# Moving the token scale of two norms behind the products in a 1024-token layer stack, with alternating block pairs and narrow sums of squares

## The chip, the cores and the metric

The kernel runs on one core of one Trainium2 chip. The core has four compute engines that run their own instruction streams: TensorE (PE in the rows, with its weight loads as PEld), VectorE (DVE), ScalarE (ACT) and GpSimd (POOL). SyncE (SP) issues the DMA transfers. The engines meet through semaphores alone. The metric is device time in microseconds (us), lower is better: the median of three runs. All arrays are float32.

## The reference, cut to what matters

Two blocks of a network stand behind each other, for one sequence of 1024 tokens with 1024 channels. The first adds four mixers of one normalized and modulated input (retention D, sliding window B, stick-breaking C, a sparse attention A). The second has a mixer block, an MLP and a gated embedding. What the change touches is this:

```python
def rms_norm(x, g):                      # rms_norm_2 is the same
    y = xf * lax.rsqrt(jnp.mean(xf * xf, axis=-1, keepdims=True) + RMS_EPS)
    return (y * g.astype(jnp.float32)).astype(x.dtype)

# first block
mod = (jax.nn.silu(c) @ w_ada + b_ada)[:, None, :]
h = rms_norm(x, norm_g) * (1.0 + scale) + shift          # opening
# stick-breaking, branch C
log_beta = jax.nn.log_sigmoid(z)
log_1m = jnp.where(mask, jax.nn.log_sigmoid(-z), 0.0)
suffix = lax.cumsum(log_1m, axis=3, reverse=True) - log_1m
a = jnp.where(mask, jnp.exp(log_beta + suffix), 0.0)
# merge, per branch
term = jax.nn.sigmoid(h @ w_merge[i]) * (yi @ w_br[i])

# second block
h = h + rms_norm_2(mix, g_mix_post[i])
hn = rms_norm_2(h, g_mlp_pre[i])                          # norm ahead of the up products
ff = jnp.square(jax.nn.relu(hn @ w_up[i])) @ w_down[i]
h = h + rms_norm_2(ff, g_mlp_post[i])
gate = jax.nn.sigmoid(rms_norm_2(h, g_ple_pre[i]) @ w_ple_gate[i])   # norm ahead of the gates
e = (p[i] @ w_ple_proj[i]) * gate
h = h + rms_norm_2(e, g_ple_post[i])
```

The factor `rsqrt(mean)` of a norm is one number for a token, the same for all channels. Call it the token scale; the gain `g` is one number for a channel.

## The kernel before, in words

**Tiles.** Activations lie transposed, channels on the 128 partitions and the 1024 tokens along the free axis, so a tensor of 1024 channels is 8 chunks of 128x1024. A dense product is computed in blocks of 128 output channels. A block has a part for each chunk of its input; a part (`three`, L609) is six matmuls of 128x512: three products (input high by weight high, input low by weight high, input high by weight low, all fp32r) for each of two token halves. A block fills one PSUM tile of 128x1024, and the tiles take two slots in turn (`slot[g % 2]`). Blocks of kind F have 8 parts and one tile, M (merge gates, and the gates g of the last stage) has 10 parts and two tiles (8 parts the gate, 2 the projection), D (down products) also two.

**Weights.** SyncE loads the weights of a block into one buffer `raw` (L543). ScalarE copies them to `whi` (L1065, L1070), which rounds them, and GpSimd subtracts for the remainder `wlo` (L1429, L1432). Both have two buffers. The split of block b+1 stands at part 0 of block b, its load at part 2.

**Inputs of a block.** A normalized chunk is split the same way: ScalarE copies it to `xhi` (L1072), and the remainder `xlo` is made by VectorE or GpSimd in turn (L1760, L1435). So each chunk passes scaling on VectorE, copy, remainder, then TensorE.

**Norms.** The channels are on the partitions, so the sum of squares over channels is a TensorE product with ones. There are two forms. The narrow form (`square_sums`, L687) has the squares as the stationary operand, eight products with one column, and leaves one 128x8 tile for the 1024 tokens; root and reciprocal are then of 128x8, and `broadcast` (L715) spreads the result to a 128x1024 row in PSUM with eight 128x128 products. The wide form (`chunk_sums`, L702) has the ones as the stationary operand and the squares as 512 moving columns, and leaves the sum already spread over partitions; root and reciprocal are then of 128x1024 (L1104, L1606). Norms of a sum that is complete before use add the eight squares on GpSimd first (`add_square`) and use one narrow sum. Norms whose input has only just been made use the wide form, chunk by chunk: the opening, and the pre-norms of MLP and gates.

**The two norms of the change.** `norm3` stands between the last block x7 of the mixer output and the up products, `norm4` between the last down products and the gates g0 to g7. Each is a post-norm (scale mm, add it to the residual `res`) with a pre-norm of the new residual behind it: narrow sum, row, scaling of mm (L1612), residual additions on VectorE for even chunks (L1624) and on GpSimd for odd ones (L1457), squares, wide sums, wide root and reciprocal, scaling of `res` with gain and token scale, split, first block. For the gates, ScalarE takes Sigmoid straight out of PSUM (L1238, L1239) and VectorE multiplies with the projection.

**Opening.** The same, with the input in place of the residual and with the modulation (`mod`), whose two vectors are products of `silu(c)` with `w_ada` (`ada_products`, VectorE, L1955; `modulation`, TensorE, L948).

**Order.** One list, TIMELINE (`list_timeline`, L192), is read by all engines: each goes through the same events and issues what is its own there. Between dense parts stand the events of attention (`spread`, L110, weighs them out). `number_tiles` (L247) numbers the PSUM tiles in the order of the blocks. In the stick stage ScalarE alternates between Exp (`ska`, L1272; `skt`, L1277) and Ln (`skt`, L1279), two functions in different table sets.

## Time and profile before

| | |
|---|---|
| median of three runs | 2966.54 us (2966.51 to 2966.85) |
| the profiled execution | 2968.03 us, of which the span in the profile is 2966.3 us |
| TensorE busy | 2697.6 us, 91% |
| VectorE, ScalarE, GpSimd busy | 949.6, 932.4, 878.7 us (32, 31, 30%) |
| chain that ended last | TensorE 79%, VectorE 9%, GpSimd 4%, ScalarE 3%, issue 3%, DMA 1% |
| copy of a block's weights to high (L1070) | 1100 ns mean |
| remainder of a block's weights (L1432) | 2531 ns mean |
| VectorE, one operation on a PSUM tile 128x1024 (L1733, L1722) | 1225 ns |
| transfers | 134.81 MB, 45 GB/s mean |

The shares of busy time are means over stages that differ. In the page's row of forty slices TensorE's busy tenths are 4 and 7 in the first two, and 6 in four later ones. The order in which to read is: the table of stretches for where TensorE idles, the chain for what a stretch costs it, and the timeline for what each engine waited for there.

### The profile page before, as it was taken

To read this page: it belongs to the slowest core of one execution; us is meant where nothing else is said; L and a number is where in the kernel's file an instruction comes from. 1 tells how busy PE (TensorE), PEld (TensorE's weight loads), DVE (VectorE), ACT (ScalarE), POOL (GpSimd) and SP (SyncE) were. 2 spreads that over 40 slices of the span, in tenths; PEclk is the share of its full clock that TensorE was granted. 3 is DMA by queue.
4 is the path that set the end of the run, shared out by engine and by line. 5 is a ranking of instruction groups with operands and counts; after the bars stand their busy time and mean duration, and the time that the engine had idled before them with its cause. 6 is when DMAs were issued, how large, how long until landed. Compare 5 with 4: busy or idle time off the path is not lost.

```text
span 2966.3 us, 29752 instructions
## 1 busy us (share of the span) xinstructions
PE 2697.6 (91%) x12244; PEld 2125.0 (72%) x12244; DVE 949.6 (32%) x1423; ACT 932.4 (31%) x1308; POOL 878.7 (30%) x497
## 2 busy tenths in 40 slices
PE   4799999999998999999988999696999999999696
PEld 2677778666687777788777777473888888888475
DVE  6212440233202454511237564406022222222512
ACT  3102441688721344421332333223211111112221
POOL 1212111343321111133642121243333322334343
PEclk9888999999997899999989999898999999999798
DMA  6101011100011000011221000110111111111011
GB/s 266 43 22 41 27 33 43 36 18 18 15 50 42 18 19 10 15 44 42 100 74 62 15 29 27 54 67 8 50 50 50 43 50 50 50 50 43 32 45 66
DMA packets 33431, 134.81 MB, mean 45 GB/s; under 512 B 3536, under 2 KB 3856, under 8 KB 32400
## 3 DMA queue, kind: packets, MB, share of 16 engines
q1 hardware_dynamic: 32976, 131.85, 12.7%
q8 instruction: 98, 1.61, 0.2%
q10 hardware_dynamic: 320, 1.05, 0.1%
q14 instruction: 37, 0.30, 0.0%
HBM read 123.45 MB, written 8.39 MB: 44 GB/s over the span
## 4 chain that ended last, share of the span: by engine, by line
PE 79%; DVE 9%; POOL 4%; ACT 3%; issue 3%; DMA 1%; SPq 0%; POOLq 0%; ACTq 0%; DVEq 0%
PE slot L613 48%; PE slot L658 12%; PE ps L826 4%; PE ps L797 3%; DVE mm L1612 2%; PE ps L775 2%; PE ps L859 1%; PE ps L850 1%; POOL wlo L1432 1%; PE ps L863 1%; PE ps L876 1%; DVE cacc L2015 1%; POOL xlo L1439 1%; DMA mm<-xT 1%; POOL pbuf L1446 1%
## 5 line engine op out<-in xcount | busy, mean ns | idle before, releaser
L613 PE MATMUL slot<-xhi,whi 128*128 128x512 f32 x2192 | 720.5, 411 | 95.8 <-DVE xlo L1764 32.9
L613 PE MATMUL slot<-xlo,whi 128*128 128x512 f32 x2192 | 693.8, 398 | 0.0
L613 PE MATMUL slot<-xhi,wlo 128*128 128x512 f32 x2192 | 690.2, 397 | 0.0
L1432 POOL TENSOR_TENSOR wlo<-raw,whi 128x1024 fp32r<-128x1024 f32 (+1 forms) x169 | 427.7, 2531 | 766.5 <-ACT whi L1070 766.5
L613 PEld LDWEIGHTS slot<-xhi,whi 128*128 128x128 f32 x2192 | 407.4, 194 | 196.0 <-issue 83.7
L613 PEld LDWEIGHTS slot<-xlo,whi 128*128 128x128 f32 x2192 | 423.3, 193 | 92.9
L613 PEld LDWEIGHTS slot<-xhi,wlo 128*128 128x128 f32 x2192 | 421.5, 192 | 92.4
L1070 ACT ACTIVATE whi<-raw 128x1024 fp32r<-128x1024 f32 (+1 forms) x169 | 185.9, 1100 | 276.4 <-PE slot L658 174.5
L658 PE MATMUL slot<-uhi,whi 128*128 128x512 f32 x512 | 158.3, 390 | 0.0
L658 PE MATMUL slot<-ulo,whi 128*128 128x512 f32 x512 | 157.8, 389 | 0.0
L658 PE MATMUL slot<-uhi,wlo 128*128 128x512 f32 x512 | 157.6, 389 | 0.0
L1507 POOL TENSOR_TENSOR ulo<-tbuf,uhi 128x1024 fp32r<-128x1024 f32 x32 | 76.6, 2395 | 226.9 <-ACT uhi L1217 226.9
L1733 DVE TENSOR_TENSOR mm<-slot,mm 128x1024 f32<-128x1024 f32 x56 | 68.6, 1225 | 229.3 <-PE slot L658 228.3
L797 PEld LDWEIGHTS ps<-brv,pbuf 128*128 128x128 f32 x936 | 127.0, 196 | 19.6 <-ACT cb L1308 5.8
L1722 DVE TENSOR_SCALAR tbuf<-slot 128x1024 f32<-128x1024 f32 x32 | 39.2, 1225 | 316.5 <-PE slot L613 316.5
L1252 ACT ACTIVATE pbuf<-ps 128x512 f32<-128x512 f32 (+3 forms) x176 | 79.5, 452 | 174.8 <-PE ps L775 173.3
L1217 ACT ACTIVATE uhi<-tbuf 128x1024 fp32r<-128x1024 f32 x32 | 33.9, 1060 | 304.3 <-DVE tbuf L1724 304.3
L1493 POOL TENSOR_TENSOR mm<-mm,zs 128x1024 f32<-128x1024 f32 x24 | 58.0, 2416 | 237.4 <-DVE zs L1646 237.4
L797 PE MATMUL ps<-brv,pbuf 128*128 128x64 f32 x936 | 122.1, 273 | 5.6 <-ACT cb L1308 3.3
L658 PEld LDWEIGHTS slot<-uhi,whi 128*128 128x128 f32 x512 | 95.5, 188 | 22.3 <-issue 3.0
L658 PEld LDWEIGHTS slot<-uhi,wlo 128*128 128x128 f32 x512 | 96.1, 188 | 20.2
L658 PEld LDWEIGHTS slot<-ulo,whi 128*128 128x128 f32 x512 | 96.1, 188 | 20.1
(301 smaller groups left out, 3223.0 us busy)
## 6 DMA issues: line engine op xcount, KB each, us to landing
raw<-wstream SPq DMA_DIRECT2D x129, 512.0 KB, 3.2
raw<-wstream SPq DMA_DIRECT2D x40, 640.0 KB, 3.8
ada<-wada SPq DMA_DIRECT2D x6, 2048.0 KB, 30.3
mm<-xT SPq DMA_DIRECT2D x1, 4096.0 KB, 24.0
mm<-xT SPq DMA_DIRECT2D x8, 512.0 KB, 3.8
res_dram<-mm SPq DMA_DIRECT2D x8, 512.0 KB, 6.2
res<-res_dram SPq DMA_DIRECT2D x8, 512.0 KB, 6.6
outT<-res SPq DMA_DIRECT2D x8, 512.0 KB, 2.6
```

Of the source, the lines that this page charges most:

```text
L613: o = mm_(outs[:, half * HALF:(half + 1) * HALF], w[b % 2][:, k_w, :], x[:, k_x, half * HALF:(half + 1) * HALF], start=first and j == 0, s ...
L658: o = mm_(slot[(g + t) % 2][:, half * HALF:(half + 1) * HALF], w[:, kc, t, :], x[:, kc, half * HALF:(half + 1) * HALF], start=kc == 0 and ...
L775: o = nc.tensor.transpose(ps6[:, (c - 4 * bi) * P:(c - 4 * bi + 1) * P], sring[m % 3][:, c * P:(c + 1) * P], t_("ident"))
L797: o = mm_(ps7[:, 0:DH], ptr[:, c * P:(c + 1) * P], v, start=c == 0, stop=c == nb - 1)
L826: o = mm_(ps4[:, c0:c1], q_[r0:r0 + DH, :], k_[r0:r0 + DH, lo * P + c0:lo * P + c1], start=j == 0, stop=j == 2)
L1070: nc.scalar.activation(flat(whi[b % 2])[:, 0:n], raw[:, 0:n], ACT.Copy).then_inc(w_hi, 1)
L1252: nc.scalar.activation(ptr[:, bi * HALF:bi * HALF + w], ps6[:, 0:w], ACT.Copy).then_inc(s_ptsb, 1)
L1432: tt(flat(wlo[b % 2])[:, 0:n], raw[:, 0:n], flat(whi[b % 2])[:, 0:n].bitcast(F32), ALU.subtract).then_inc(w_lo, 1)
L1493: tt(mm[:, n, :], mm[:, n, :], zs[0][:], ALU.add).then_inc(sum_done, 1)
L1507: tt(ulo[:, n, :], tbuf[n % 2][:], uhi[:, n, :].bitcast(F32), ALU.subtract).then_inc(u_lo, 1)
L1612: v.scalar_tensor_tensor(out=dst, in0=src, scalar=g, in1=row, op0=ALU.mult, op1=ALU.mult).then_inc(s_, 1)
L1733: v.tensor_tensor(mm[:, n, :], slot[gg % 2][:], mm[:, n, :], ALU.add).then_inc(slot_free[gg % 2], 1)
```

## The change

What it does, in five parts:

1. **Pairs.** The first two blocks behind a norm are issued alternately: part i of the first, then part i of the second for i up to 3, then the rest. The pairs are Dv0/Dv1, o0/o1, Ecb0/Eca0, x0/x1, u0_0/u0_1 and g0/g1 (`opened`, `opened_gates`). The weights of the second block are split at the norm instead of at part 0 of the first, and those of block 1 are loaded right behind those of block 0 (ahead of the tables and of the last modulation weights). The residual's load moves from part 0 of x1 to part 3. The tiles of g0 and g1 are renumbered: g0 has tiles t and t+2, g1 has t+1 and t+3.
2. **Token scale behind the products.** In `norm3` and `norm4` the chunks that go into the products carry the gain alone: `xhi` is a ScalarE copy of `res` scaled by the gain, `xlo` a VectorE operation with gain and subtraction, and all eight residual additions are GpSimd's. The squares of the chunks are summed in narrow form, one after each of the eight rounds of the pair (`hsum`); root, reciprocal and the row (`hrow`, ahead of the second block's last two parts) follow while products run. The row is copied to `wide_row`. For the up blocks the evacuation becomes max(x, 0) times the row. For the gates VectorE multiplies tile by row (`scale_gate`, at part 7), ScalarE takes Sigmoid of that in place, and VectorE multiplies with the projection.
3. **Sums.** All sums of squares are in narrow form. The sums of a complete tensor take two accumulators: GpSimd's sum of seven, and the last square straight from ScalarE.
4. **Opening.** Chunk sums in narrow form, root and reciprocal of 128x8, then the row by eight products. VectorE's reciprocal stands between its product 3 and 4 of the modulation's second half. Chunk squares use three buffers in place of two.
5. **Tables.** `preload_act_table_set("natural_log_exp_and_others")` at the start of the stick stage and behind each gate Sigmoid of branch B: one set that holds both functions.

Where the order moves, from the instruction streams of the two kernels. First TensorE in the opening, ahead of the first weight block (L948 and L986 are the modulation, sbuf and pbuf hold squares, slot is a block's tile). Before:

```order
L948 MATMUL ps<-tab,ada_sum_102 128x1 x8
L709 MATMUL ps<-sbuf_72,tab 128x512 x2
L709 MATMUL ps<-sbuf_73,tab 128x512 x2
L709 MATMUL ps<-sbuf_72,tab 128x512 x2
L709 MATMUL ps<-sbuf_73,tab 128x512 x2
L709 MATMUL ps<-sbuf_72,tab 128x512 x2
L709 MATMUL ps<-sbuf_73,tab 128x512 x2
L709 MATMUL ps<-sbuf_72,tab 128x512 x2
L709 MATMUL ps<-sbuf_73,tab 128x512 x2
L948 MATMUL ps<-tab,ada_sum_101 128x1 x8
L613 MATMUL slot<-xhi,whi_56 128x512 x2
```

After:

```order
L986 MATMUL ps<-tab,ada_sum_102 128x1 x8
L731 MATMUL ps<-tab,sbuf_72 128x1 x8
L731 MATMUL ps<-tab,sbuf_73 128x1 x8
L731 MATMUL ps<-tab,pbuf_74 128x1 x8
L731 MATMUL ps<-tab,sbuf_72 128x1 x8
L731 MATMUL ps<-tab,sbuf_73 128x1 x8
L731 MATMUL ps<-tab,pbuf_74 128x1 x8
L731 MATMUL ps<-tab,sbuf_72 128x1 x8
L731 MATMUL ps<-tab,sbuf_73 128x1 x8
L757 MATMUL ps<-tab,rrms 128x128 x8
L986 MATMUL ps<-tab,ada_sum_101 128x1 x8
L653 MATMUL slot<-xhi,whi_56 128x512 x2
```

The eight wide matmuls are eight groups of eight one-column ones, and the row's broadcast stands ahead of the second modulation.

Next TensorE at the norm ahead of the up products, from the row's sum on (whi_57 and whi_56 are the weights of u0_0 and u0_1). Before:

```order
L690 MATMUL ps<-tab,pbuf_74 128x1 x8
L720 MATMUL ps<-tab,rrms 128x128 x8
L709 MATMUL ps<-sbuf_72,tab 128x512 x2
L709 MATMUL ps<-sbuf_73,tab 128x512 x2
L709 MATMUL ps<-sbuf_72,tab 128x512 x2
L709 MATMUL ps<-sbuf_73,tab 128x512 x2
L709 MATMUL ps<-sbuf_72,tab 128x512 x2
L709 MATMUL ps<-sbuf_73,tab 128x512 x2
L709 MATMUL ps<-sbuf_72,tab 128x512 x2
L709 MATMUL ps<-sbuf_73,tab 128x512 x2
L613 MATMUL slot<-xhi,whi_57 128x512 x2
L613 MATMUL slot<-xlo,whi_57 128x512 x2
```

After:

```order
L731 MATMUL ps<-tab,pbuf_74 128x1 x8
L731 MATMUL ps<-tab,sbuf_73 128x1 x8
L757 MATMUL ps<-tab,rrms 128x128 x8
L653 MATMUL slot<-xhi,whi_57 128x512 x2
L653 MATMUL slot<-xlo,whi_57 128x512 x2
L653 MATMUL slot<-xhi,wlo_59 128x512 x2
L653 MATMUL slot<-xhi,whi_56 128x512 x2
L653 MATMUL slot<-xlo,whi_56 128x512 x2
L653 MATMUL slot<-xhi,wlo_58 128x512 x2
L731 MATMUL ps<-tab,sbuf_72 128x1 x8
L653 MATMUL slot<-xhi,whi_57 128x512 x2
L653 MATMUL slot<-xlo,whi_57 128x512 x2
```

The eight wide sums that stood ahead of the first product are gone from there; behind each round of the two blocks stands a narrow sum.

Last ScalarE in the stick stage, about a Sigmoid of the merge gates (zs). Before:

```order
L1272 ACT_TABLE_LOAD
L1272 ACTIVATE ska_81<-ps 128x128
L1277 ACTIVATE skt_79<-skt_79 128x384
L1279 ACT_TABLE_LOAD
L1279 ACTIVATE skt_79<-skt_79 128x384
L1169 ACT_TABLE_LOAD
L1169 ACTIVATE zs_108<-slot 128x1024
L1070 ACTIVATE whi_56<-raw 128x1280
L1272 ACT_TABLE_LOAD
L1272 ACTIVATE ska_82<-ps 128x256
L1277 ACTIVATE skt_80<-skt_80 128x512
L1279 ACT_TABLE_LOAD
```

After:

```order
L1303 ACTIVATE ska_81<-ps 128x128
L1308 ACTIVATE skt_79<-skt_79 128x384
L1310 ACTIVATE skt_79<-skt_79 128x384
L1203 ACT_TABLE_LOAD
L1203 ACTIVATE zs_108<-slot 128x1024
L1205 ACT_TABLE_LOAD
L1112 ACTIVATE whi_56<-raw 128x1280
L1303 ACTIVATE ska_82<-ps 128x256
L1308 ACTIVATE skt_80<-skt_80 128x512
```

The table loads at every change between Exp and Ln are gone; a Sigmoid has its own load ahead of it and one behind it. In all the built program has 154 table loads before and 67 after.

The diff, cut to its core:

```diff
+OPENERS = [("Dv0", "Dv1"), ("o0", "o1"), ("Ecb0", "Eca0"), ("x0", "x1"), ("u0_0", "u0_1")]
+SECOND = {b for _, b in OPENERS} | {"g1"}
...
+def opened(events, a, b):
+
+    first, second = dense_part_events([a]), dense_part_events([b])
+    at = events.index(first[0])
+    rest = [ev for ev in events if ev not in first and ev not in second]
+    pair = []
+    for i, ev in enumerate(first):
+        pair.append(ev)
+        if i < 4:
+            pair.append(second[i])
+        if a == "u0_0":
+            pair.append(("hsum", 4, i))
+    pair += second[4:]
+    if a == "u0_0":
+        pair.insert(-2, ("hrow", 4))
+    return rest[:at] + pair + rest[at:]
...
+def opened_gates(events):
+
+    g0, g1 = dense_part_events(["g0"]), dense_part_events(["g1"])
+    at = events.index(g0[0])
+    rest = [ev for ev in events if ev not in g0 and ev not in g1]
+    pair = []
+    for i in range(8):
+        pair.append(g0[i])
+        if i < 4:
+            pair.append(g1[i])
+        pair.append(("hsum", 6, i))
+    pair += g1[4:6] + [("hrow", 6)] + g1[6:8] + g0[8:] + g1[8:]
+    return rest[:at] + pair + rest[at:]
...
+            g += {"g0": 1, "g1": 3}.get(name, 2 if kind in "MD" else 1)
...
+            load_weights(1)
...
+            def column_sum(k, accs, place=0):
+
                 if place == 0:
                     pe.wait_ge(nstd, k)
-                square_sums(place, acc, place == 0, True).then_inc(nsum, 1)
-
-            def chunk_sums(k, j):
-
-                if k:
+                for m, (acc, sem_, n) in enumerate(accs):
+                    pe.wait_ge(sem_, n)
+                    o = square_sums(place, acc, place == 0 and m == 0, m == len(accs) - 1)
+                o.then_inc(nsum, 1)
+
+            def chunk_sum(k, j, n):
+
+                if k and n == 0:
                     pe.wait_ge(nstd, k)
-                for n in range(NC):
-                    pe.wait_ge(pq_done, 8 * j + n + 1)
-                    for half in range(2):
-                        o = mm_(sum_banks(k)[half], t_("ones"), sbuf[n % 2][:, half * HALF:(half + 1) * HALF],
-                                start=n == 0, stop=n == 7)
-                    if n < 7:
-                        o.then_inc(pq_used, 1)
-                o.then_inc(nsum, 1)
+                pe.wait_ge(pq_done, 8 * j + n + 1)
+                square_sums(0, sring[n % 3], n == 0, n == 7).then_inc(pq_used if n < 7 else nsum, 1)
...
             modulation(1)
-            chunk_sums(0, 0)
+            for n in range(NC):
+                chunk_sum(0, 0, n)
+            broadcast(0)
             modulation(0).then_inc(mod_mm, 1)
...
+                        act.preload_act_table_set("natural_log_exp_and_others")
...
+                    if ev[2] == 7 and BLOCKS[ev[1]][1][0] == "g":
+                        n = int(BLOCKS[ev[1]][1][1])
+                        act.wait_ge(g_scaled, n + 1)
+                        nc.scalar.activation(zs2[n % 2][:], zs2[n % 2][:], ACT.Sigmoid).then_inc(g_sig, 1)
...
+                    wait_tile(act, LAST_USE[4 if k == 3 else 5])
+                    split_weights(INDEX["u0_1" if k == 3 else "g1"])
                     for n in range(NC):
                         wait_residual(act, int(k == 5), n)
+                        nc.scalar.activation(xhi[:, n, :], res[:, n, :], ACT.Copy,
+                                             scale=v_("g_mlp_pre" if k == 3 else "g_ple_pre", n, 1)).then_inc(x_hi, 1)
                         chunk_square(1 if k == 3 else 2, n, res[:, n, :])
-                    std(k + 1)
-                    wait_tile(act, LAST_USE[4 if k == 3 else 5])
-                    for n in range(NC):
-                        act.wait_ge(x_src, 16 + 8 * (k == 5) + n + 1)
-                        split_wide(n, mm[:, n, :])
                     if k == 5:
                         act.wait_ge(p_in, 32)
                         for n in range(2):
                             nc.scalar.activation(yhi[:, n, :], zs2[n][:], ACT.Copy).then_inc(y_hi, 1)
+                    std(k + 1)
...
+            def add_residual(k, n):
+                pool.wait_ge(t_ready, 8 * k + n + 1)
+                tt(res[:, n, :], res[:, n, :], mm[:, n, :], ALU.add).then_inc(res_odd if n % 2 else res_added, 1)
...
-                    v.tensor_scalar(t[:], slot[g % 2][:], 0.0, None, ALU.max).then_inc(slot_free[g % 2], 1)
+                    v.scalar_tensor_tensor(out=t[:], in0=slot[g % 2][:], scalar=0.0, in1=wide_row,
+                                           op0=ALU.max, op1=ALU.mult).then_inc(slot_free[g % 2], 1)
...
+            def scale_gate(name):
+
+                n, g = int(name[1]), TILE[name]
+                wait_tile(dve, g)
+                if n < 2:
+                    dve.wait_ge(y_lo, 10)
+                v.tensor_tensor(zs2[n % 2][:], slot[g % 2][:], wide_row, ALU.mult).then_inc(slot_free[g % 2], 1)
+                wait_evacuated(dve, name)
+                v.tensor_copy(token[:, 0:1], token[:, 1:2]).then_inc(g_scaled, 1)
...
+                    if (t, kc) == (0, 4):
+                        dve.wait_ge(nstd, 1)
+                        v.reciprocal(rrms[:, 0, :], rms[:, 0, :]).then_inc(nrstd, 1)
...
-                    add_residual(k, (k - 3) // 2, post)
-                    applied(k, t_ready, 8 * (k - 1) // 2)
-                    row = rstd(k + 1)
-                    for n in range(NC + 1):
+                    row, first = rstd(k), 8 * (4 if k == 3 else 5)
+                    for n in range(NC + 2):
                         if n < NC:
-                            wait_residual(dve, (k - 3) // 2, n)
-                            scaled(mm[:, n, :], res[:, n, :], v_(pre, n, 1), row, x_src)
-                        if n:
-                            split_wide(4 if k == 3 else 5, n - 1, n - 1, mm[:, n - 1, :])
-                    applied(k + 1, x_src, 24 + 4 * (k - 3))
+                            scaled(mm[:, n, :], mm[:, n, :], v_(post, n, 1), row, t_ready)
+                        if n == NC:
+                            applied(k, t_ready, 8 * (k - 1) // 2)
+                        m = n - 2
+                        if m >= 0:
+                            dve.wait_ge(x_hi, first + m + 1)
+                            v.scalar_tensor_tensor(out=xlo[:, m, :], in0=res[:, m, :], scalar=v_(pre, m, 1),
+                                                   in1=xhi[:, m, :].bitcast(F32), op0=ALU.mult, op1=ALU.subtract
+                                                   ).then_inc(x_lo if m % 2 else x_lo2, 1)
+                    v.tensor_copy(wide_row, rstd(k + 1)).then_inc(napplied, 1)
+                    dve.wait_ge(napplied, k + 2)
```

## Rows read from the trace of the kernel before

**Rows 1.** Table of stretches: stretch and us, busy us of each engine, clock, DMA, GB/s.

```profile
core 0: us, PE busy (x) PEld busy (x) DVE busy (x) ACT busy (x) POOL busy (x), PEclk, DMA share, GB/s
555.00:800.00 245.00, 237.21 (x947) 153.82 (x948) 75.65 (x132) 204.84 (x247) 98.81 (x109) 0.97 0.06 21
1527.00:1540.00 13.00, 11.77 (x56) 9.01 (x56) 7.62 (x8) 7.90 (x8) 9.54 (x4) 1.00 0.01 1
1999.00:2066.00 67.00, 38.12 (x111) 22.27 (x110) 45.29 (x28) 22.15 (x23) 22.23 (x9) 0.80 0.02 6
2758.00:2830.00 72.00, 39.60 (x114) 22.77 (x112) 46.51 (x29) 22.57 (x23) 28.76 (x11) 0.79 0.07 24
```

**Rows 2.** The chain that ended last: start us, length us, engine, tile, line.

```profile
27.79 16.04 PE ps L709 x32
...
79.68 11.20 PE slot L613 x48
...
2070.50 32.92 PE slot L613 x144
...
2147.02 43.52 PE slot L613 x192
...
2830.39 99.81 PE slot L613 x432
```

**Rows 3.** Timeline of the opening: start, length, operation, in brackets the idle before.

```profile
22.44 3.54 PE L948 MATMUL ps<-tab,ada_sum 128*128 128x1 f32 x16 [22.44 <-DVE ada_sum L1955]
...
36.56 5.25 DVE L1955 SCALAR_TENSOR_TENSOR ada_sum<-ada,csil,ada_sum 128x1024 f32<-128x1024 f32 x4 [0.26 <-DMA ada<-wada]
...
43.66 1.84 PE L948 MATMUL ps<-tab,ada_sum 128*128 128x1 f32 x16
...
52.83 2.48 DVE L2026 SCALAR_TENSOR_TENSOR mm<-mm,gmul,pbuf 128x1024 f32<-128x1024 f32 x2
```

**Rows 4.** Table of stretches: mixed work behind a wait; narrow products alone.

```profile
578.00:588.20 10.20, 9.25 (x19) 5.93 (x20) 2.86 (x4) 5.53 (x7) 6.46 (x4) 0.50 0.17 49
919.00:926.20 7.20, 7.20 (x72) 7.13 (x71) 0.00 (x0) 0.02 (x1) 0.00 (x0) 0.50 0.22 86
```

**Rows 5.** Groups by line and form, ScalarE, 540 to 810: busy and mean ns, idle before.

```profile
L1279 ACT ACT_TABLE_LOAD x48 | 61.6, 1283 | 0.9
```

**Rows 6.** Timeline of the stick stage, TensorE behind a Sigmoid.

```profile
578.95 1.19 PE L613 MATMUL slot<-xhi,whi 128*128 128x512 f32 x2 [3.38 <-ACT zs L1169]
...
779.70 1.19 PE L613 MATMUL slot<-xhi,whi 128*128 128x512 f32 x2 [3.75 <-ACT zs L1169]
```

**Rows 7.** Waits, 555 to 800: engine, line, waited for: total us, times, longest.

```profile
PE ps L859 <- DVE skt L1848: 2.1, 1, 2.1
```

**Rows 8.** Timeline about the second norm and the mixer output (x0, x1).

```profile
1538.51 1.95 PE L720 MATMUL ps<-tab,rrms 128*128 128x128 f32 x16
...
1893.55 3.31 DVE L1703 TENSOR_TENSOR zs<-zs 128x1020 f32<-128x1020 f32 x1
...
1932.03 1.06 ACT L1070 ACTIVATE whi<-raw 128x1024 fp32r<-128x1024 f32 x1 [6.07 <-DMA raw<-wstream]
```

**Rows 9.** Timeline of the norm ahead of the up products.

```profile
2005.79 3.58 PE L690 MATMUL ps<-tab,pbuf 128*128 128x1 f32 x16 [4.62 <-POOL pbuf L1446]
...
2009.96 3.78 PE L720 MATMUL ps<-tab,rrms 128*128 128x128 f32 x16 [0.59 <-DVE rrms L1603]
...
2017.59 2.35 POOL L1457 TENSOR_TENSOR res<-res,mm 128x1024 f32<-128x1024 f32 x1 [11.85 <-DVE mm L1612]
2018.73 2.28 DVE L1624 TENSOR_TENSOR res<-res,mm 128x1024 f32<-128x1024 f32 x1
...
2038.50 6.55 DVE L1606 RECIPROCAL pbuf<-pbuf 128x1024 f32<-128x1024 f32 x1 [6.70 <-ACT pbuf L1104]
```

**Rows 10.** Timeline of the norm ahead of the gates, and of the last norm.

```profile
2767.43 3.78 PE L720 MATMUL ps<-tab,rrms 128*128 128x128 f32 x16 [0.73 <-DVE rrms L1603]
...
2935.01 3.57 PE L690 MATMUL ps<-tab,pbuf 128*128 128x1 f32 x16 [4.82 <-POOL pbuf L1446]
```

164 lines of the change are left out of this document (79 added, 85 removed).

## The prediction

> **What bounds the kernel now.** I read the table of stages first. In it the reader sees which stages leave TensorE idle: 28.9 us of the 67 ahead of the MLP and 32.4 us of the 72 behind it are idle, while the stage of the stick-breaking attention (555 to 800) has only 7.8 idle in 245 though ScalarE is busy for 205 [rows 1]. So TensorE is the bound everywhere but in the norms. The chain of waits comes next, for the price of a block: four blocks of 8 parts take 43.52 us, 10.88 each, 1.36 us a part at full clock [rows 2]. Then the order of time at each norm shows what ends last.
>
> **Opening.** Now the eight chunk sums are 16.04 us of TensorE [rows 2], the first scaled chunk starts at 52.83 [rows 3], and the second block starts at 79.68 and takes about 11.0, to 90.7 [rows 2]. After, a chunk sum is eight products with one column. The same form takes 3.54 us in the cold and 1.84 just behind wide products [rows 3]. Which of the two holds is the first question. The trace has 7.2 us of nothing but narrow products, TensorE and its weight loads busy all the time, and the clock is granted at 0.50 throughout, 1.2 GHz of 2.4 [rows 4]. So I take the cold price: 8 x 3.44 (3.54 less the overlap) = 27.5, from 27.8 to 55.4. Root and reciprocal end at 56.0. VectorE has held back four of its products behind that reciprocal, 5.25 us [rows 3], to 61.4; the modulation's products follow cold, 3.54, to 65.0, and 0.9 of small operations: the first scaled chunk is at 65.9, 13 later than now. The row of the root stands in PSUM then, so scaling shares no port with GpSimd's subtractions; and the second block's first four parts fill the gaps between chunks. First product 3.9 later, 12 products at 1.2 GHz 5.1, then 13 us to the end of the first block's part 7 and 5.5 for the second's last four with what the gaps cost: 28.1, so the pair ends at 94.0. **Term: +3.3.** If the sums ran at 1.84 the same steps give 52.2 + 28.1 = 80.3, -10.4; that is the other end.
>
> The Trainium skill ("TensorE: Matmul & The Clock Gate", section "What's actually happening") says that sustained matmul activity releases the throttle, whatever the number of products. By it the narrow sums would warm up as the wide ones did. This trace speaks against it for narrow ones; I keep it as a rival. By the rows the whole change comes to -59.4, by the rule to 13.7 less, -73.1.
>
> **Stick-breaking attention.** The built program has 154 table loads before and 67 after; the 95 that alternate between exp and log (48 of them here [rows 5], 1.28 us each) become one at the start and one behind each gate's Sigmoid. Nearly all of that lies under TensorE, which is the bound there. What it can return are the places where TensorE waits: 3.38 us at 578.95 and 3.75 at 779.70, both for a Sigmoid that stands behind a log load and its own [rows 6]. One load less there, and a shorter queue ahead, gives 1.9 and 1.4; one wait of 2.1 for VectorE's mask behind a log [rows 7] gives about 1.3. The first wait also drops the clock, for some 10 us of mixed work [rows 4], worth 5, and the second one for 3.4, worth 1.7. With all of the clock it is 11.3, with none 4.6. **Term: -9.**
>
> **Other pairs.** For o0/o1, GpSimd's weight remainder (2.4) now stands ahead of its four chunk remainders, and TensorE waits for it instead of for the chunk: 0, within 1. For the pair after the second norm the idle time between chunks is filled (1.2 idle in 13 us [rows 1], 2 over the whole pair), and the doubled narrow sums (four for two) start 4.8 earlier and end 0.3 earlier: **-2.3**. For x0/x1 the third weight block no longer waits behind the residual's load (GpSimd's weight remainder there ended 1.7 us after TensorE was free; ScalarE shows the wait for the DMA [rows 8]): -1.7; but GpSimd gets one more operation in the stretch where VectorE is already stopped by each (3.31 for a 1.22 operation [rows 8]): +2.2, on the path to the wait for the pool product. **+0.5**, from -1.7 to +2.5.
>
> **Norm ahead of the up products.** Now: x7 ends at 2001.2; sum starts 4.62 later, row broadcast at 2009.96 for 3.78, ready 2013.8; residual, chunk sums, a wide reciprocal of 6.55 [rows 9], scaling, and the second block starts at 2070.50 [rows 2], ends 2081.45. After, step by step:
> - ScalarE squares x7 from PSUM, 1.06; the sum of the other seven starts at once, warm 1.8, then the last square's 1.8, behind wide products. Root, reciprocal: row broadcast at 2005.7, cold 3.8: T0 = 2009.45, 4.3 earlier.
> - GpSimd adds all eight chunks, 2.35 each. In the rows VectorE's two-operand SBUF addition of 1.22 takes 2.28 beside it [rows 9]: the two exclude each other. VectorE's remainder (1.2) is such an operation, so a chunk costs 3.5, the first is ready at T0 + 7.2, the last by +32.
> - TensorE: at 1.2 GHz the first pair takes 5.1, its sum 2.0; then three rounds of two parts and a sum, 2.72 + 1.8 = 4.55; four of one part and a sum, 3.2: the last sum ends at +41.0. The chunks come faster than that from the second on, so TensorE sets the time, and between narrow sums it has wide parts enough that I take the full clock. Two parts 2.8, the row 1.8 warm (1.95 at 1538.51 [rows 8]), two parts 2.7: the second block ends at T0 + 48.3 = 2057.8.
> - The row's copy (1.22) and the first scaled evacuation (1.28) end at +47.9, just under the last two parts; third block's weights at +44.9. In the MLP the scaling adds 0.06 to a VectorE operation that waits for TensorE: nothing.
>
> **Term: 2057.8 - 2081.45 = -23.7.** The stages behind need no new wait.
>
> **Norm ahead of the gate products.** T0 comes from 2771.25 (the broadcast at 2767.43 plus 3.8 [rows 10]) to 2767.1, 4.15 earlier. The same 48.3; then the projection parts of g0 and g1, 2.75 each, to +53.8. GpSimd's narrow remainders, for which TensorE waits now, are done by +38. One wait is new: ScalarE must split g2's weights before g0's Sigmoid, and that split waits for g0's second tile at +51.0. Then 1.26, a table load 1.28, Sigmoid 1.03, the product 1.23 (what such operations take on these engines), gaps 0.3: g2 starts at +56.1, 2.3 after TensorE is free, = 2823.2. Now g2 starts 6 x 13.6 before the end of 2830.39 + 99.81 [rows 2], at 2848.5. **-25.3.** The other six gates run as now: scaling frees the first slot 1.3 us after its tile, the other tile takes 2.7.
>
> **Tail.** The sum of the first seven is ready, the last square comes 2.75 after TensorE's end instead of 4.82 of wait [rows 10] for GpSimd as well; two sums instead of one. First row of the result 2.0 to 3.6 earlier: **-2.9**.
>
> **Sum:** 3.3 - 9 - 2.3 + 0.5 - 23.7 - 25.3 - 2.9 = -59.4. The profiled execution took 2968.03 with a span of 2966.3; less 59.4 it is 2908.6, and 2907.1 from the median of 2966.54, which I predict as 2907.
>
> **Rivals.**
> - Narrow sums warm the clock in the opening (10.4 gained, not 3.3 lost): 2893.4. For it: the same form ran in 1.84 in this very place now, if behind wide products [rows 3]. Against: the clock of 0.50 under narrow products alone [rows 4]. 7%.
> - The eight additions and eight remainders hold each other up as the scalings and subtractions do now, a chunk each 5.6 us instead of 3.5: the last remainder at +46, then sum, two parts, row, two parts: 57, 8.7 later in both norms: 2907.1 + 17.4 = 2924.5. For it: all eight additions are now on the slower engine. Against: the blocked operation waits for one partner only. 12%.
> - Table loads don't pay (TensorE is full there): 2907.1 + 4.4 = 2911.5, inside the forecast.
> - Slower: a clock that narrow sums among wide parts hold at 1.2 GHz, at both pairs. Rounds then cost 5.12 + 3.44 and 2.56 + 3.44: 34.2 + 24.0 after +7.3, four parts 10.2 and the row 3.8: +79.5 where now it is +72.0, so 7.5 lost, and 8.3 lost before g2; the mixed rows of the stick stage stay slow too, 4.6 gained only. 3.3 - 4.6 - 2.3 + 0.5 + 7.5 + 8.3 - 2.9 = +9.8: 2976.3. It decides from where both pairs are in the low state for over 70% of their time. For it: the same row [rows 4]. Against: each round has a part or two of six wide products. 4%.
>
> **Numbers.** Forecast 75% (2898 to 2917), warm opening 7%, slow chunks 12%, slow clock 4%; 2% for something unseen. Range 2893 to 2927. A change of 0.2% is 5.9 us, about what a measurement tells from none. Faster 0.95, same 0.02, slower 0.03.
>
> **What would show it.** Eight narrow sums at 3.4 each with the clock at 0.50 in the opening, and the first scaled chunk near 66. Second block of the pair ended at 48 behind the row in both norms, no TensorE wait over 1 us in them but the first, clock 1.00 from about 5 us in. g2 2.3 us late. About 20 ScalarE table loads in the stick stage, its length 236. It is wrong if TensorE waits for remainders of a chunk past the second, or if the narrow sums inside the pairs are at 3.4.

## The result, and the profile after

The changed kernel takes 2914.81 us, the median of 4 runs from 2913.77 to 2916.03, against 2966.69 (2966.51 to 2970.18) for the kernel before in the same session. The ratio is 0.9818 with a 95% interval of 0.9806 to 0.983: 52 us gained where 59.4 were predicted (2907), inside the range of 2893 to 2927. The profiled execution has a span of 2913.8 us, 52.5 less than before, so 6.9 of the 59.4 are missing in it.

To see where it came from I cut both traces at ten points that both kernels have, the starts of ScalarE's copies of the weights of ten blocks, and took the difference of each of the eleven stages. In the same stages I added up from the clock records how long TensorE's clock was at its low level. The records begin at 31.9 us before and at 60.3 after, so what was low ahead of that is not in the first row.

| stage | before, low | after, low | change | forecast |
|---|---|---|---|---|
| start to Dk1 (opening) | 91.8, 13.7 | 95.9, 10.2 | +4.1 | +3.3 |
| Dk1 to Bm2 (retention, sliding window, first steps of stick-breaking) | 486.9, 68.9 | 483.5, 61.4 | -3.4 | 0 |
| Bm2 to Aq0 (stick-breaking) | 249.0, 13.0 | 243.2, 6.8 | -5.8 | -9 |
| Aq0 to Cm7 (A's attention) | 365.8, 81.9 | 368.0, 81.9 | +2.2 | 0 |
| Cm7 to o3 | 247.3, 6.8 | 247.4, 3.4 | +0.2 | 0 |
| o3 to Ek1 (second norm) | 212.5, 30.7 | 210.0, 30.7 | -2.6 | -2.3 |
| Ek1 to Ep1 (forgetting attention) | 193.2, 10.2 | 198.7, 20.5 | +5.5 | 0 |
| Ep1 to x4 | 102.3, 27.3 | 101.2, 27.3 | -1.1 | +0.5 |
| x4 to d0_0 (norm ahead of up) | 147.2, 27.3 | 123.2, 13.7 | -24.0 | -23.7 |
| d0_0 to g3 (norm ahead of gates) | 754.8, 34.1 | 730.5, 13.7 | -24.3 | -25.3 |
| g3 to the end | 115.4, 29.6 | 112.2, 27.2 | -3.2 | -2.9 |

From x4 on, the two late norms and the tail gave 51.5 where the sum has 51.9. Of the 6.9 that are missing, 6.5 lie ahead of x4: 1.0 was gained there where the sum has 7.5. Most of that is in attention stages whose work on TensorE the change leaves as it is.

First the opening, in the timeline of the changed kernel (start, length, operation, idle before):

```profile
34.71 3.55 PE L731 MATMUL ps<-tab,pbuf 128*128 128x1 f32 x16
...
55.86 7.16 DVE L2006 SCALAR_TENSOR_TENSOR ada_sum<-ada,csil,ada_sum 128x1024 f32<-128x1024 f32 x4
...
55.99 3.79 PE L757 MATMUL ps<-tab,rrms 128*128 128x128 f32 x16 [0.66 <-DVE rrms L1999]
...
63.07 2.98 PE L986 MATMUL ps<-tab,ada_sum 128*128 128x1 f32 x16 [3.29 <-DVE ada_sum L2006]
...
71.16 1.19 PE L653 MATMUL slot<-xhi,whi 128*128 128x512 f32 x2 [5.12 <-DVE xlo L2086]
...
94.36 1.04 PE L717 MATMUL slot<-tab,zs 128*128 128x128 f32 x8
```

A narrow sum takes 3.55 us by itself and 3.44 in the row of eight, and the pair is done at 94.36 where 94.0 was forecast. That the two agree so well is in part luck: VectorE's four products behind the reciprocal took 7.16 and not 5.25 (one of them takes 3.26 in the chain of waits, while GpSimd makes the weight remainder below), so the first scaled chunk came at 67.17 and not at 65.9, and from there the pair took 27.2 and not 28.1.

```profile
56.66 2.63 POOL L1472 TENSOR_TENSOR wlo<-raw,whi 128x1024 fp32r<-128x1024 f32 x1 [56.15 <-ACT whi L1112]
```

The chain of waits answers to the wide sums of [rows 2] with one piece, which holds all eight sums:

```profile
27.87 27.48 PE ps L731 x128
...
71.16 23.38 PE slot L653 x96
```

Three signs were named wrongly. The stick stage was to take 236 us with about 20 table loads of ScalarE; from Bm2 to Aq0 it takes 243.2, with 14 (90 before). And I had said that the clock column would read 0.50 in the opening. It reads 1.00, because this trace has no clock record before 60 us:

```profile
28.00:55.00 27.00, 27.00 (x128) 27.00 (x128) 4.61 (x4) 8.27 (x8) 0.00 (x0) 1.00 0.31 132
64.00:74.00 10.00, 4.88 (x17) 4.25 (x18) 7.59 (x10) 5.06 (x6) 4.35 (x2) 0.50 0.98 325
```

The durations tell the level: 3.55 for the form that takes 1.84 at the high clock [rows 3]. So the clock was low through 27 us of narrow products with TensorE busy all the time. In the kernel before, the first record, at 31.9 us, is a high one, 4.1 us into the wide sums. The Trainium skill ("TensorE: Matmul & The Clock Gate", section "What's actually happening") has it that activity releases the throttle; for these narrow products the trace disagrees.

The norm ahead of the up products, against [rows 9]:

```profile
2000.24 1.84 PE L731 MATMUL ps<-tab,pbuf 128*128 128x1 f32 x16
...
2001.94 3.03 PE L731 MATMUL ps<-tab,sbuf 128*128 128x1 f32 x16
...
2005.56 3.78 PE L757 MATMUL ps<-tab,rrms 128*128 128x128 f32 x16 [0.59 <-DVE rrms L1645]
...
2010.81 24.62 POOL L1494 TENSOR_TENSOR res<-res,mm 128x1024 f32<-128x1024 f32 x8 [2.17 <-DVE mm L1651]
...
2014.37 2.17 DVE L2130 SCALAR_TENSOR_TENSOR xlo<-res,vec,xhi 128x1024 fp32r<-128x1024 f32 x1 [1.32 <-ACT xhi L1432]
...
2016.69 1.19 PE L653 MATMUL slot<-xhi,whi 128*128 128x512 f32 x2 [7.35 <-DVE xlo L2130]
...
2020.87 1.84 PE L731 MATMUL ps<-tab,sbuf 128*128 128x1 f32 x16
```

The first sum stands right behind x7 instead of 4.62 us later. The second one is slower than worked out, 3.03 and not 1.8: the clock records have the low level from 2002.5 on. So the row starts 5.2 behind x7's end where it was 8.8, 3.6 sooner and not 4.3. The first product comes 7.35 behind the row, the clock is high again from 2019.6, and TensorE waits for nothing more: the pair ends 47.0 behind the row (48.3 forecast), because the clock rose 2.9 us into the pair and not after 5. GpSimd's eight additions and VectorE's remainders give a chunk about every 3.3 us (3.5 was worked out); the "slow chunks" rival (5.6) is out, and so is the slow clock: sums among wide parts take 1.84. The wait at the gates came too, 2.49 where 2.3 was forecast:

```profile
2793.35 1.27 ACT L1112 ACTIVATE whi<-raw 128x1280 fp32r<-128x1280 f32 x1 [10.04 <-PE slot L653]
...
2794.64 1.28 ACT L1326 ACT_TABLE_LOAD   x1
...
2797.09 1.22 DVE L1777 TENSOR_TENSOR mm<-slot,zs 128x1024 f32<-128x1024 f32 x1 [5.21 <-ACT zs L1326]
...
2798.46 0.70 PE L653 MATMUL slot<-xhi,whi 128*128 128x512 f32 x2 [2.49 <-DVE mm L1777]
```

In the stick stage the two waits of [rows 6] are 1.49 and 2.48 now, and the wait for VectorE of [rows 7] has stayed, where 1.3 of it was to go:

```profile
578.20 0.70 PE L653 MATMUL slot<-xhi,whi 128*128 128x512 f32 x2 [1.49 <-ACT zs L1203]
```

```profile
772.74 0.70 PE L653 MATMUL slot<-xhi,whi 128*128 128x512 f32 x2 [2.48 <-ACT zs L1203]
```

```profile
PE ps L897 <- DVE skt L1896: 2.1, 1, 2.1
```

### The profile page after: what moved, and what is told of

The parts are those of the page before. It is cut to its first block, busy times and chain, and to the rows that moved or that the text cites. A ratio compares the mean times of both kernels' runs of the same rounds, so it can differ in the third digit from the quotient of the medians.

```text
span 2913.8 us, 30462 instructions
## 1 busy us (share of the span) xinstructions
PE 2709.8 (93%) x12660; PEld 2179.4 (75%) x12660; DVE 922.2 (32%) x1431; ACT 817.1 (28%) x1218; POOL 872.8 (30%) x492
## 4 chain that ended last, share of the span: by engine, by line
PE 87%; DVE 6%; ACT 3%; POOL 2%; issue 2%; DMA 1%; SPq 0%; POOLq 0%; ACTq 0%; DVEq 0%
PE slot L653 54%; PE slot L699 12%; PE ps L864 4%; PE ps L835 3%; PE ps L731 3%; PE ps L813 2%; PE ps L897 1%; PE ps L888 1%; PE ps L901 1%; PE ps L914 1%; DVE cacc L2068 1%; DMA mm<-xT 1%; DVE ada_sum L2006 1%; PE ps L757 1%; POOL wlo L1472 1%
## 5 line engine op out<-in xcount | busy, mean ns | idle before, releaser
L1759 DVE SCALAR_TENSOR_TENSOR tbuf<-slot,tab 128x1024 f32<-128x1024 f32 x32 | 39.2, 1224 | 302.4 <-PE slot L653 302.3
```

## The experiments

Eleven runs: the changed kernel once more, and ten further versions. The kernel before was run beside each group: medians of 2968.2 to 2968.7, with single runs between 2965 and 2978. Single runs of one kernel lie up to 14 us apart, so a difference of a few us between two medians says little; what an edit did is read from the stages. Stage lengths below are from one profile each.

| run | us, median (range) | ratio to before, 95% |
|---|---|---|
| e1_again | 2919.8 (2913.8 to 2921.5) | 0.9828 (0.9814 to 0.9841) |
| e2_tables_off | 2928.4 (2920.4 to 2932.4) | 0.9851 (0.9836 to 0.9866) |
| e3_tables_only | 2971.8 (2960.2 to 2974.5) | 1.0002 (0.9991 to 1.0012) |
| e4_ug_in_row | 2929.6 (2924.6 to 2936.8) | 0.9866 (0.9849 to 0.9883) |
| e5_late_by_3 | 2916.1 (2915.6 to 2917.1) | 0.9821 (0.9808 to 0.9835) |
| e6_sigmoid_first | 2914.8 (2914.2 to 2916.7) | 0.9817 (0.9804 to 0.9831) |
| e7_even_on_vector | 2923.0 (2922.0 to 2925.5) | 0.9844 (0.9831 to 0.9858) |
| e8_pair_sums | 2904.7 (2901.2 to 2908.8) | 0.9783 (0.9767 to 0.9798) |
| e9_rounded_sums | 2887.6 (2886.1 to 2892.4) | 0.9724 (0.971 to 0.9738) |
| e10_combined | 2881.7 (2880.0 to 2888.0) | 0.9707 (0.9691 to 0.9723) |
| e11_before_late | 2973.2 (2969.6 to 2978.4) | 1.0016 (1.0007 to 1.0025) |

### Where the 6.5 us missing ahead of x4 went: e1, e2, e3, e5, e11

Two theories are tried here. Theory P (phase): the records of TensorE's clock change only at the points of one even raster, which has no fixed place in the program, and what a short wait costs depends on where it lies against that raster. "0.45 us behind a point" below is the distance of a stage's start from the last such point. Rival C (the change): something that the change leaves behind makes the stages longer.

**e1_again**, no edit.

> The changed kernel as it is, once more. Open is why the stages between the opening and the mixer's output gave 1.0 us in the first profile where the prediction has 7.5: by the first profile the sparse attention of branch A (blocks Cm2 to Cm7) was 2.4 us longer than before and the forgetting attention (Ek1 to Ep1) 5.5 us longer, though not an instruction of theirs was changed. Theory P (phase): TensorE's clock falls and rises on a grid of its own, and these stages have short waits that cost one interval or two, as they fall on it; then this execution may show either length, and the time is 2914.8 within 2. Rival C (the change): something that the change leaves behind makes the stages longer, the forgetting attention is 198 to 199 us from the copy of Ek1's weights to that of Ep1's here as well, 193.2 before. A time of 2913 to 2917 by both.

The stages repeat: A's attention from Cm2 to Cm7 233.5 (233.6 in the first profile, 231.1 before), the forgetting attention 198.5. That fits both theories, since both executions started the forgetting attention 0.45 us behind a point of the raster. The median was 5 higher than in the first session, with one run at 2913.8; the profiled execution was longer in the opening, from Dk1 to Bm2, from d0_0 to g3 and in the last stage, 1.3 to 1.7 us each.

**e2_tables_off** takes the two requests for the table set out of the changed kernel, and **e3_tables_only** puts the same lines into the kernel before.

```diff
                     if name[0] == "B":
-                        act.preload_act_table_set("natural_log_exp_and_others")
 ...
-                if s == 0:
-                    act.preload_act_table_set("natural_log_exp_and_others")
```

> The changed kernel without its two requests for the exp/log table set (part 5 undone, all else stays). By the first profile, stick-breaking gave 5.8 us from block Bm2 to Aq0 instead of 9. Theory: the waits for two Sigmoids are 1.3 to 1.9 us longer again, and the clock falls for 10 us behind the first: 5.8 us are lost in the stick stage, 2920.6, and between 2919 and 2923 with what the other attention stages make of the new phase. Rival: table loads lie under TensorE and pay for nothing but what the two waits show directly, 2.3 us, 2917. Rival: my forecast of 9 was right and was lost again behind the stage: 2924. Theory P also says: as everything behind the stick stage moves by an amount that is no multiple of the clock's interval, the forgetting attention takes a different length than in e1_again (193 to 199 us); rival C says it stays.

> The kernel before with the two requests for the exp/log table set and nothing else. Theory: 4.6 to 8 us gained in the stick stage, so 2959 to 2962. Rival (table loads hidden under TensorE): within 1.5 us of before, 2965 or more. Rival C about the forgetting attention: if the table set left behind were its cause, that stage would be 198 us instead of 193.2 here too, and the gain would all but vanish, 2964 to 2966; theory P leaves it anywhere from 193 to 199.

The table of stretches, from Bm2 to Aq0, of e1, e2 and e3:

```profile
581.90:825.08 243.18, 240.71 (x979) 157.62 (x979) 74.74 (x121) 96.38 (x156) 98.09 (x97) 0.99 0.06 21
```

```profile
582.93:831.85 248.92, 244.58 (x983) 160.68 (x984) 73.04 (x121) 193.73 (x232) 97.91 (x97) 0.97 0.06 20
```

```profile
577.63:820.80 243.17, 240.70 (x979) 157.59 (x979) 74.72 (x121) 96.37 (x156) 98.09 (x97) 0.99 0.06 21
```

ScalarE's busy time halves, from 193.7 to 96.4, and the stage gives 5.7 to 5.8 of it, the same in both kernels. The first steps of stick-breaking stand ahead of Bm2, and 12 of the table loads with them: there the requests give 0.5 more (Bm1 to Bm2 29.5 for 30.0). My theory of 5.8 holds for the stage, neither rival does. For the whole it does not: the median of e2, 2928.4, is above all three forecasts, and e3 took 5.8 us out of the kernel before and is no faster (its span 2.7 longer), because its forgetting attention took 200.2 instead of 193.2 and A's attention 233.6 instead of 231.1. In the changed kernel the same edit is worth 8.7 by the medians (e2 against e1) and 10.8 by the profiled spans, the stage's 5.7 and 3.8 between Cm7 and o3 (251.2 against 247.4) among it. So much of the price of an edit was set behind it. Without the requests the forgetting attention was at its longest, 200.7: the table set left behind is not the cause there. For A's attention these two runs can't tell: it took 231.1 to 231.2 in the three profiles without the requests and 233.5 to 233.6 in nine of the ten with them, and the starts differ in the same way, 2.0 to 2.1 and 2.3 to 2.4 us behind a point. The tenth speaks for the start: e8 changes the opening alone, starts this stage 3.2 behind a point and takes 236.1. Before, after, e8:

```profile
962.40:1193.52 231.12, 215.25 (x1136) 173.44 (x1136) 106.67 (x280) 99.18 (x204) 39.15 (x35) 0.90 0.05 15
```

```profile
957.01:1190.56 233.55, 217.55 (x1136) 175.27 (x1136) 106.15 (x280) 99.20 (x203) 39.16 (x35) 0.89 0.04 15
```

```profile
947.78:1183.84 236.06, 219.98 (x1136) 176.85 (x1136) 106.12 (x280) 99.36 (x204) 39.20 (x35) 0.88 0.04 15
```

**e5_late_by_3** and **e11_before_late** add the same work to the changed kernel and to the kernel before.

```diff
+                if name == "Ek1" and part == 0:
+                    for _ in range(14):
+                        mm_(slot[g % 2][:, 0:HALF], whi[b % 2][:, 0, :], xhi[:, 0, 0:HALF], start=True, stop=True)
```

> The changed kernel with 14 extra products of 128x512 (0.227 us each, 3.2 us in all, overwritten at once) in TensorE's stream at the head of block Ek1, just ahead of the forgetting attention. [...] 3.2 us later the changed kernel stands at 0.45 + 3.2 - 3.41 = 0.2, so the stage is near the short length, 193.2 to 195.5 plus the 3.2 of extra work: 196.4 to 198.7, no longer than the 198.5 without it, though 3.2 us of work were added. Rival C (the change has made the stage longer by itself): 198.5 + 3.2 = 201.7. The whole time follows: 2916 to 2920 by P, 2922 to 2923 by C, against the 2919.8 of e1_again.

> The kernel before with the same 14 extra products (3.2 us) at the head of block Ek1 that cost the changed kernel nothing in e5_late_by_3. Theory P (what counts is where the forgetting attention lies against the clock's grid): the kernel before starts it 0.07 us behind a point of the grid, its shortest place (193.2 us). 3.2 us later is 3.2 behind a point, where e2 and e3 (3.34 and 3.10) took 200.7 and 200.2: 200.2 to 200.7 and the 3.2 of work, 203.4 to 204, so the same 3.2 us of work cost 10 here, and the kernel takes 2975 to 2979. Rival (the extra wide products kept TensorE busy in e5 and so shortened the low stretch by themselves): they would do so here as well, and the stage would be no longer than 193.2 + 3.2 = 196.4, the kernel at most 3.2 slower, 2970 to 2972.

The starts that both expectations speak of, in the profiles up to then: 0.07 us behind a point in the kernel before (193.2 us), 0.45, 0.45 and 0.49 in the changed kernel, e1 and e4 (198.4 to 198.7), 3.10 and 3.34 in e3 and e2 (200.2 and 200.7). In the sum for e5 the 3.2 us carry the start past the next point, from where the distance counts anew. The stretch from Ek1 to Ep1, the kernel before first, then the changed kernel, e5 and e11:

```profile
1653.33:1846.53 193.20, 183.51 (x986) 146.19 (x986) 106.25 (x184) 66.15 (x143) 33.07 (x34) 0.97 0.07 25
```

```profile
1647.99:1846.69 198.70, 189.06 (x988) 150.54 (x988) 106.21 (x184) 66.15 (x143) 33.05 (x34) 0.95 0.08 24
```

```profile
1647.77:1846.16 198.39, 188.75 (x1002) 150.19 (x1001) 106.22 (x184) 66.13 (x142) 33.13 (x34) 0.97 0.07 24
```

```profile
1652.82:1854.87 202.05, 192.40 (x1003) 153.22 (x1003) 106.37 (x185) 66.19 (x143) 33.18 (x34) 0.95 0.07 24
```

In this stage 14 more products cost the changed kernel nothing, and the kernel before 8.9 us. What they change is the clock. Far behind them, at the second low stretch of the stage, the changed kernel has it low for two steps in a row and e5 for one:

```profile
1726.05:1729.46 3.41, 3.24 (x15) 3.24 (x16) 2.32 (x3) 0.31 (x2) 0.59 (x1) 0.50 0.48 154
1729.46:1732.87 3.41, 3.41 (x14) 2.67 (x13) 1.89 (x5) 1.67 (x5) 0.10 (x1) 0.50 0.00 0
```

```profile
1729.20:1732.61 3.41, 3.41 (x15) 2.68 (x13) 2.34 (x7) 1.67 (x5) 0.04 (x1) 0.51 0.13 52
1732.61:1736.03 3.42, 3.42 (x24) 3.06 (x23) 0.08 (x1) 0.00 (x0) 0.42 (x1) 0.99 0.00 0
```

The stage has three places where waits and narrow products let the clock fall. In these records it falls and rises at points that are not tied to the program, and a place costs one step or two as it lies against them (in e3 and e2, which start 3.10 and 3.34 us behind a point, the second place costs three). The extra products stand ahead of the first place only and end 57 us ahead of the second, too far to have kept TensorE busy there; and in e11 they made the low time longer (20.5 against 10.2). For the forgetting attention theory P is shown, rival C and the rival of e11 are out: shifted to the start that the changed kernel has, the kernel before takes the changed kernel's length. My number for e11 was 1.5 too high: this execution came to the stage 0.68 us behind a point of the clock instead of 0.07. The 3.2 us of work take it past the next point to 0.44, where the stage took 197.8 to 198.8 in eight other profiles; 198.8 + 3.2 = 202.0, and 202.05 was measured. The Trainium skill says as much ("TensorE: Matmul & The Clock Gate", section "What's actually happening"): what watches TensorE runs freely and does not start with the kernel. It speaks there of a kernel's first products and puts the cost of their warm-up under 1% of a typical span; here the effect comes in the middle of the kernel and is 5.5 us in one stage, a tenth of what the change brings.

In e11 the whole time is a weaker witness: its median is 5.0 above the kernel before, 2973.2, between what the rival gives (up to 2972) and what P gives (2975 or more), with single runs from 2969.6 to 2978.4.

### What bounds the late pairs: e4, e7, e6

**e4_ug_in_row**.

```diff
-        if i < 4:
+        if i < 4 and a != "u0_0":
             pair.append(second[i])
 ...
-    pair += second[4:]
+    pair += second if a == "u0_0" else second[4:]
```

and the same for g0 and g1.

> The changed kernel with the blocks of the two late pairs (u0_0 then u0_1, g0 then g1) in a row instead of alternating; the narrow sums stay one behind each part of the first block, and the row stays ahead of the second block's last two parts. Theory (TensorE is the bound of the pair from the second chunk on: 16 parts 21.8, eight sums 14.7, a row 1.95 and the cold start 2.4 fill it): one part and a sum take 3.2 us and a chunk comes every 3.3, so the first block ends at about 34 to 36 behind the row and the second 12.8 later, 47 to 49 us as with alternation (48.4 measured): within 1.5 us a norm, 2912 to 2918. Rival: alternation is what fills the wait for chunks, and without it four parts (5.4 us) are lost in each norm: 2925.6. Rival: with one part a round narrow products prevail and the clock falls: a round 6.0 instead of 3.2, over 15 us a norm lost: 2945.

Ahead of the up products both blocks end 47.0 behind the row, as with alternation: for the pair itself the theory holds, and neither rival does. But the kernel takes 2929.6, well outside the theory's 2912 to 2918 (by the time alone, the rival with 2925.6 would have seemed right). The stage is 9.3 us longer, and TensorE waits behind the pair:

```profile
2060.12 1.06 ACT L1250 ACTIVATE uhi<-tbuf 128x1024 fp32r<-128x1024 f32 x1 [13.57 <-DVE tbuf L1760]
2061.09 1.04 ACT L1110 ACTIVATE whi<-raw 128x1024 fp32r<-128x1024 f32 x1
...
2064.65 2.33 POOL L1470 TENSOR_TENSOR wlo<-raw,whi 128x1024 fp32r<-128x1024 f32 x1
...
2067.04 1.22 PE L651 MATMUL slot<-xhi,whi 128*128 128x512 f32 x2 [7.97 <-POOL wlo L1470]
```

With the blocks in a row, the split of the third block's weights comes behind the evacuation of u0_0 in ScalarE's and GpSimd's streams, and that evacuation now waits for the row. I had not seen this. Ahead of the up products alternation is worth 0 by filling gaps and 9 by where it puts the next block's weights: a wait of 8.0, and a clock that is low for 20.5 us of the stage instead of 13.7. At the gates it is worth nothing in this profile: the stage up to g3 takes 731.1 (730.5 and 731.9 in the two profiles of the changed kernel), and the last one 110.8 (112.2 and 113.9).

**e7_even_on_vector**.

```diff
                             scaled(mm[:, n, :], mm[:, n, :], v_(post, n, 1), row, t_ready)
+                            if n % 2 == 0:
+                                dve.wait_ge(t_ready, 8 * ((k - 3) // 2) + n + 1)
+                                v.tensor_tensor(res[:, n, :], res[:, n, :], mm[:, n, :], ALU.add
+                                                ).then_inc(res_added, 1)
```

> The changed kernel with the residual additions of the even chunks back on VectorE, in both late norms (GpSimd keeps the odd ones), all else as changed. In the profile of the changed kernel a chunk comes every 3.3 us: GpSimd's addition 2.35, and VectorE's remainder, held until it ends. Theory (TensorE sets the pair's time from the second chunk on): only the first chunk matters, VectorE adds it in 1.2 instead of GpSimd in 2.35, so the first product comes 1.1 us sooner and each pair ends 1.1 sooner, 2.2 in all. Rival (VectorE becomes the bound: per two chunks it has two scalings, an addition, and two remainders of which each waits for GpSimd, 2.5 + 1.2 + 4.4 = 8.1 us against 6.6 now): later chunks come every 4.0 us and the pair ends 2 to 4 us later.

Slower by 2.3 in the stage ahead of up and by 1.3 to 2.7 in the next. That is the rival's amount, but by another mechanism than either had:

```profile
2017.00 2.35 DVE L2129 TENSOR_TENSOR res<-res,mm 128x1024 f32<-128x1024 f32 x1
...
2019.27 1.27 DVE L2136 SCALAR_TENSOR_TENSOR xlo<-res,vec,xhi 128x1024 fp32r<-128x1024 f32 x1
...
2020.69 1.19 PE L653 MATMUL slot<-xhi,whi 128*128 128x512 f32 x2 [8.69 <-DVE xlo L2136]
```

The first chunk is added sooner, but its remainder stands behind the third chunk's addition in VectorE's stream, and that takes 2.35 beside GpSimd's: the first product comes 8.69 behind the row, not 7.35, and the clock is low for 17.1 us of the stage, not 13.7. Afterwards TensorE waits for nothing, so the later chunks were no bound. The median is 8 above that of the changed kernel in the first session; the two stages explain 4 to 5 of it.

**e6_sigmoid_first**.

```diff
-                    if ev[2] == 0 and ev[1] + 1 < nblocks and BLOCKS[ev[1] + 1][1] not in SECOND:
+                    if (ev[2] == 0 and ev[1] + 1 < nblocks and BLOCKS[ev[1] + 1][1] not in SECOND
+                            and BLOCKS[ev[1]][1] != "g1"):
 ...
                         nc.scalar.activation(zs2[n % 2][:], zs2[n % 2][:], ACT.Sigmoid).then_inc(g_sig, 1)
+                        if n == 1:
+                            split_weights(ev[1] + 1)
```

> The changed kernel with one move: ScalarE splits the weights of g2 behind the Sigmoids of g0 and g1 instead of ahead of them. In the profile of the changed kernel g2's first product waits 2.5 us for VectorE's product of g0, which waits for that Sigmoid. Theory: the Sigmoid of g0 is done at +1.1 behind VectorE's scaling, before TensorE is through with g1, and the wait for the product goes to under 0.5 us; g2's weights then end last, 4.2 us behind the end of g0's second tile, that is before g1's second tile is through: 2.0 to 2.5 us gained in the stage. Rival: the split then comes after the second Sigmoid and g2 waits for its weights instead (GpSimd's remainder takes 2.9 behind the copy's 1.3): nothing gained, within 0.5 us.

```profile
2797.33 0.73 PE L653 MATMUL slot<-xhi,whi 128*128 128x512 f32 x2 [1.70 <-POOL wlo L1475]
```

The Sigmoid is out of the way, and GpSimd's remainder of g2's weights is what ends last: a wait of 1.70 instead of 2.49. The stage is 1.3 shorter, between theory and rival; the whole time shows nothing of it. In the changed kernel that remainder had ended only 0.8 ahead of the first product.

### What the narrow sums cost: e8, e9, e10

**e8_pair_sums**, the opening alone; the diff shows the two main parts.

```diff
-            for n in range(NC):
-                chunk_sum(0, 0, n)
-            broadcast(0)
+            for n in range(4):
+                pe.wait_ge(pp_added, n + 1)
+                square_sums(0, (sbuf[0], pbuf[0])[n % 2], n == 0, n == 3).then_inc(pp_used if n < 3 else nsum, 1)
             modulation(0).then_inc(mod_mm, 1)
+            broadcast(0)
 ...
+            for n in range(4):
+                pool.wait_ge(pq_done, 2 * n + 2)
+                a, b_ = sbuf if n % 2 == 0 else pbuf
+                tt(a[:], a[:], b_[:], ALU.add).then_inc(pp_added, 1)
```

> The changed kernel with another opening: GpSimd, idle there, adds the squares of two chunks (2.4 us each), TensorE takes four narrow sums instead of eight, VectorE's last four modulation products stand ahead of the reciprocal, and the second modulation ahead of the row. Theory (narrow sums at 3.44 us each in the cold bound the opening, 27.5 us in the profile of the changed kernel): sums from 31.1 to 44.9 at 3.44 each, modulation to 48.4, row to 52.2, first product at about 56 to 57 instead of 71.2, 14 to 15 us gained at the first product and 13 to 15 at the end of the pair: 2903 to 2906. Rival: the first weight block, whose remainder GpSimd makes behind its additions, and the load of the second block behind that, come last, and the second block waits: 10 gained. Rival: the sums are not the bound but the modulation's weights (they land at 31.6 and 36.5) with VectorE's eight products, done at 42: 10 or less.

```profile
58.98 1.19 PE L654 MATMUL slot<-xhi,whi 128*128 128x512 f32 x2 [4.99 <-DVE xlo L2096]
```

The first product came at 58.98 instead of 71.16, 12.2 sooner, and the opening stage took 84.7 instead of 95.9: 11.2 gained, between the theory's 13 to 15 and the 10 of the rivals. Two of GpSimd's additions took 3.2 to 3.3 us beside VectorE's products, and the sums ended at 46.9, not 44.9. VectorE's own eight products ended at 46.9 too, so with four sums the two are level and the sums are no longer the only bound. The edit moves several things at once; that the eight sums bounded the opening is shown better by e9, which changes them alone. The median of 2904.7 fits the theory's 2903 to 2906, but the single runs lie between 2901.2 and 2908.8, and in the profiled one, the longest, A's attention takes 2.5 more than in the changed kernel.

**e9_rounded_sums**, opening and both late norms.

```diff
-                nc.scalar.activation(sring[n % 3][:], src, ACT.Square).then_inc(pq_done, 1)
+                nc.scalar.activation(sring_r[n % 3][:], src, ACT.Square).then_inc(pq_done, 1)
 ...
+                one, step = (ones_r[:], 2) if rounded else (t_("ones", 0, 1), 1)
```

> The changed kernel with the chunk squares of the opening and of the two late norms written by ScalarE as fp32r, and summed by fp32r products with two columns of ones instead of fp32 with one (the squares are rounded, nothing else). Theory (a narrow sum costs its weight loads: fp32 takes two passes of eight, 3.44 us in the cold and 1.84 warm, and fp32r one): 1.7 us cold and 0.9 warm. Opening: eight sums 14 instead of 27.5, so the row is at 43 and VectorE's last four modulation products end last, at 48, with modulation and scaling the first product is at 56 instead of 71.2: 14 to 15 gained. In each late norm chunks, one every 3.3 us, set the pair's time: it ends 40 to 42 us behind the row instead of 47: 5 to 7 gained each. In all 24 to 29 less than 2915 to 2920, with 6 for what the clock does in the attention stages: 2886 to 2898. Rival (the cost of a narrow product is a fixed one of some 110 to 220 ns however it is loaded): nothing gained. Rival (TensorE no longer has enough to do in the pair, so its clock falls there): the opening gains, the norms don't, 2903.

```profile
27.61 13.78 PE L735 MATMUL ps<-ones_r,sr 128*128 128x2 f32 x64 [1.91 <-ACT sr L1137]
```

```profile
2007.30 1.19 PE L655 MATMUL slot<-xhi,whi 128*128 128x512 f32 x2 [7.35 <-DVE xlo L2137]
...
2015.13 0.95 PE L735 MATMUL ps<-ones_r,sr 128*128 128x2 f32 x8
...
2035.25 1.95 PE L761 MATMUL ps<-tab,rrms 128*128 128x128 f32 x16
```

A sum is 1.72 us cold and 0.95 warm, half of both; the opening took 82.8 (13.2 less, and the sums 13.7 less), and the late stages 7.1 and 7.0 less. The clock did not fall in the pairs. An fp32 sum stands as 16 products in the trace, an fp32r sum as 8, and each takes 215 ns cold in both: the cost of a narrow sum goes with the number of its passes, and both rivals are out. What a pass spends, the load of its stationary operand or something else, these runs don't separate. One part of the theory was wrong: chunks do not set the pair's time here either. It ends 39.9 behind the row with no wait of TensorE but the first, so TensorE is still the bound.

**e10_combined**: e9 with the products ahead of the reciprocal, the modulation ahead of the row, and the edit of e6.

```diff
-                    if (t, kc) == (0, 4):
-                        dve.wait_ge(nstd, 1)
-                        v.reciprocal(rrms[:, 0, :], rms[:, 0, :]).then_inc(nrstd, 1)
 ...
+            dve.wait_ge(nstd, 1)
+            v.reciprocal(rrms[:, 0, :], rms[:, 0, :]).then_inc(nrstd, 1)
```

> e9_rounded_sums with three more moves in one: in the opening VectorE's last four modulation products ahead of the reciprocal and the second modulation ahead of the row, and at the gates the two Sigmoids ahead of the split of g2's weights (the move of e6_sigmoid_first, which gave 1.1). Theory: with sums that end at about 43 the products no longer have to wait for the root: first product at 53 to 54, 2 to 3 earlier than in e9, and 1 at the gates: 3 to 4 less than e9. Rival (the four products end at the same time as the root anyway, so their place is worth nothing): 1 less than e9.

```profile
53.64 23.72 PE slot L655 x96
```

The first product is at 53.64, 4.0 sooner than in e9 (57.61), where 2 to 3 were expected, and the kernel takes 2881.7, the fastest of all: 33 us below the changed kernel's first median, with the squares of three norms rounded to fp32r. It is 5.9 below e9, more than the 3 to 4 expected. Of the 9.6 between the two profiled spans 4.0 are the opening and 2.0 the last stage; 3.5 lie between Cm7 and o3 (247.5 for 250.9), where the edit changes nothing.

## Why the prediction was right, and where not

- **Late norms** (-23.7 and -25.3; measured -24.0 and -24.3). The mechanism held, and its largest steps by their numbers: 7.35 from the row to the first product, a chunk every 3.3, sums at 1.84, the wait of g2 2.49 for 2.3. Two steps were off and cancelled: the row came 3.6 and 3.0 sooner behind the last block and not 4.3 and 4.15, since the second sum runs at the low clock (3.03 and 2.99, not 1.8), and the pairs took 47.0 and not 48.3, since the clock rose 2.9 us into them. That TensorE is the bound is shown by e4, and by e9, which halved the sums and gained 7 in each. No run undid the token scale behind the products by itself; that it is what took the wide sums, root and reciprocal off the path is read from the rows.
- **Opening** (+3.3; +4.1). Cold narrow sums at 3.44 were the right price, and e9 shows that they bounded it. VectorE's four products were mis-sized (7.16, not 5.25); what followed was quicker than worked out, so that the pair's end is off by 0.4 alone.
- **Stick stage** (-9; -5.8 from Bm2, and 0.5 more ahead of it). The term was mis-sized. Two waits gave 3.2 (3.3 worked out). The low clock behind the first Sigmoid, 10.2 us, vanished as forecast. The 1.3 at VectorE's mask was wrong: that wait is 2.1 us before and after. And the low clock behind the second Sigmoid grew from 3.4 to 6.8 us where I had it vanish.
- **Other pairs** (0, -2.3, +0.5; +0.2, -2.6, -1.1). The first and the last are within their bounds, the second 0.3 from its size. In the last, 1.7 us were to be gained at the third weight block; the trace before has TensorE idle for 0.91 there, not 1.7. The x pair's shift of GpSimd's work was not tried alone.
- **Not in the sum at all**: three stages that I took as 0. They gave +4.3 together (-3.4, +2.2, +5.5). For the forgetting attention (+5.5) the cause is shown by e5 and e11: where it comes to lie against the clock's changes. For A's attention (+2.2) it is likely from the lengths that went with the start in all 13 profiles, e8 above all, and was not tried by a shift alone. From Dk1 to Bm2 (-3.4), 0.5 are the table loads. 3.0 lie between Dm0 and Dm4, in the sliding window's attention (80.8 and 77.8 us, with the clock low for 13.7 and 6.8); that this too is the clock's phase is argued only. Over the whole stage less low time does not go with less time: e1 has 58.0 us low and takes 484.7, the changed kernel's first profile 61.4 and 483.5, e3 61.4 and 486.2.

## What to carry to other kernels

The time of a stage in which TensorE's clock falls at short waits can depend on where the stage starts, by up to 7.5 us here. So compare an edit stage by stage before you believe the total: an edit that took 5.8 us out of its own stage was worth 0 in one kernel and 8.7 in the other. Products with one or two columns are paid by the pass, however little each one multiplies; ask first whether there can be fewer passes, or whether the squares can be summed ahead: halving the passes was worth 27 us, at the price of rounded squares. And where an order is changed, follow the weights of the block behind, since alternation earned its 9 us there, in one of two places, and not where it was put.

## What the runs showed of the hardware that I had not expected

- 27 us of products with one column, without a pause, ran at TensorE's low clock from first to last; the clock's records start late in a trace (at 31.9 and 60.3 us), and until then only durations tell (3.55 against 1.84 us).
- The forgetting attention took 193.2 us when it started 0.07 us behind a point of the clock's raster, 197.8 to 198.8 at 0.43 to 0.49, and 200.2 and 200.7 at 3.10 and 3.34.
- An fp32r sum of 128x1024 squares with two columns takes 0.95 us warm, the fp32 form with one column 1.84.
- Half of ScalarE's work in a stage (97 us of 76 table loads, 1.28 us each) was worth 5.7 us.
